# ScalarE copies the weights' high halves, and rotations, pool sums and three half projections take new places in a two-layer decoder trunk

## What is computed

```
h = rmsnorm(x); z = h @ w_in            # rq rk rv rg | pu | mq mk mv mo mi mf
y_ret  = silu(rg) * head_norm(retention(rope(rq), rope(rk), rv))   # 6 heads of 64
y_pool = (windowed mean of pu, widths 2 4 8 16, minus pu) @ w_pool # 4 groups of 64
y_ml   = sigmoid(mo) * head_norm(mlstm(conv(mq, mk), mv, mi, mf))  # 4 heads, 8 chunks
x = x + [y_ret, y_pool, y_ml] @ w_out
x = x + (silu(g) * u) @ w_down          # g, u = rmsnorm(x) @ w_gate_up
x = x + sigmoid(rmsnorm(x) @ w_ple_gate) * (p @ w_ple_proj)
```

## Time and profile before

| | us |
|---|---|
| time, median of 3 runs (range) | 2586.88 (2586.88 to 2587.53) |
| the profiled execution's own time | 2588.19 |
| its span, first to last instruction | 2586.4 |
| TensorE busy in the span | 2499.7 |
| VectorE busy | 1459.0 |
| GpSimd busy | 1288.7 |
| ScalarE busy | 713.5 |
| mean granted TensorE clock | 0.985 |

### The profile page before, as it was taken

The page is one execution under the profiler, slowest core; times in us unless marked ns, Lnnn a source line. Parts: engine busy times, 40 slices in busy tenths (PEclk is TensorE's granted clock), DMA queues, the critical chain, the costliest instruction groups (busy, mean ns, idle before and its releaser), DMA issues.

```text
span 2586.4 us, 29552 instructions
## 1 busy us (share of the span) xinstructions
PE 2499.7 (97%) x11844; PEld 2061.5 (80%) x11844; DVE 1459.0 (56%) x1746; ACT 713.5 (28%) x1091; POOL 1288.7 (50%) x739
## 2 busy tenths in 40 slices
PE   7999998999999999999899999899999999999996
PEld 5887876888888888887778878678888888888885
DVE  6977747663334362354776876677434333534546
ACT  4110114343333330014222021323333333211232
POOL 4423322468788764444434323323787887544430
PEclk9999998999999999999999999999999999999998
DMA  4322222122222352211132112221222323422111
GB/s 154 94 61 54 67 66 92 41 90 74 82 90 74 88 197 105 75 49 49 47 122 83 49 45 71 77 69 62 72 84 79 93 74 97 162 104 78 49 42 65
DMA packets 62904, 208.64 MB, mean 81 GB/s; under 512 B 8872, under 2 KB 17320, under 8 KB 58416
## 3 DMA queue, kind: packets, MB, share of 16 engines
q1 hardware_dynamic: 32544, 116.41, 14.9%
q10 hardware_dynamic: 30224, 90.35, 10.1%
HBM read 161.08 MB, written 32.54 MB: 75 GB/s over the span
## 4 chain that ended last, share of the span: by engine, by line
PE 93%; DVE 4%; ACT 1%; issue 1%; POOL 0%; DMA 0%; ACTq 0%; DVEq 0%
PE proj L1735 19%; PE proj L1736 19%; PE proj L1737 19%; PE proj L1829 5%; PE proj L1830 5%; PE proj L1831 5%; PE aux L1829 5%; PE aux L1830 5%; PE aux L1831 5%; PE aux L1962 1%; PE aux L1971 1%; DVE ret_t L898 1%; PE aux L1873 1%; PE aux L2028 1%; PE aux L1952 0%
## 5 line engine op out<-in xcount | busy, mean ns | idle before, releaser
L1682 POOL TENSOR_TENSOR w_hi<-w_raw,zero 128x1024 fp32r<-128x1024 f32 (+1 forms) x145 | 278.1, 1918 | 1057.3 <-PE proj L1737 1046.1
L1735 PE MATMUL proj<-h_hi,w_hi 128*128 128x512 f32 x1792 | 712.9, 398 | 28.2 <-DVE h_lo L601 17.0
L1736 PE MATMUL proj<-h_hi,w_lo 128*128 128x512 f32 x1792 | 701.6, 392 | 0.0
L1737 PE MATMUL proj<-h_lo,w_hi 128*128 128x512 f32 x1792 | 701.6, 392 | 0.0
L1735 PEld LDWEIGHTS proj<-h_hi,w_hi 128*128 128x128 f32 x1792 | 338.8, 189 | 104.4 <-issue 28.9
L1686 POOL TENSOR_TENSOR w_lo<-w_raw,w_hi 128x1024 fp32r<-128x1024 f32 (+1 forms) x145 | 390.2, 2691 | 11.4
L1737 PEld LDWEIGHTS proj<-h_lo,w_hi 128*128 128x128 f32 x1792 | 338.6, 189 | 71.6
L1736 PEld LDWEIGHTS proj<-h_hi,w_lo 128*128 128x128 f32 x1792 | 339.1, 189 | 70.7 <-issue 2.9
L971 DVE TENSOR_TENSOR x<-x,proj 128x512 f32<-128x512 f32 x128 | 87.7, 687 | 315.0 <-PE proj L1737 315.0
L1693 POOL TENSOR_TENSOR w_lo<-w_raw,w_hi 128x512 fp32r<-128x512 f32 x120 | 183.6, 1531 | 97.5 <-ACT w_hi L1283 97.5
L1693 POOL TENSOR_TENSOR w_lo<-turns,w_hi 128x512 fp32r<-128x512 f32 x120 | 180.4, 1504 | 62.9 <-ACT w_hi L1283 62.9
(11 more groups left out here) (271 smaller groups left out, 4296.3 us busy)
## 6 DMA issues: line engine op xcount, KB each, us to landing
w_raw<-weights SPq DMA_DIRECT2D x170, 512.0 KB, 3.6
act_spill<-act ACTq DMA_DIRECT2D x44, 512.0 KB, 5.5
turns<-weights SPq DMA_DIRECT2D x40, 512.0 KB, 4.3
h_whole<-act_spill ACTq DMA_DIRECT2D x12, 1024.0 KB, 8.8
ffn_b_whole<-act_spill ACTq DMA_DIRECT2D x8, 1024.0 KB, 6.0
ret_t<-ret_qkv ACTq DMA_DIRECT2D x48, 128.0 KB, 3.9
w_raw<-weights SPq DMA_DIRECT2D x16, 384.0 KB, 3.0
x<-x_in ACTq DMA_DIRECT2D x8, 512.0 KB, 8.6
```

The source lines that it names most:

```text
L1682: g.tensor_tensor(whi[:, slot, 0:n], w, zero1[:, 0:1].to_broadcast([P, n]), ALU.add).then_inc(w_hi_made, 1)
L1735: pe.matmul(out, wh, rhi, start=first, stop=False)
L1736: pe.matmul(out, wl, rhi, start=False, stop=False)
L1737: return pe.matmul(out, wh, rlo, start=False, stop=final)
```

## The change

Four edits, in both layers:

1. **High parts of the weights on ScalarE** (in the diff `units_high`). From the fourth unit of the first layer on, ScalarE copies raw weights to `w_hi`; GpSimd waits for that copy and only subtracts. The copies stand at fixed places in ScalarE's list, mostly two units ahead of TensorE.
2. **Halves around the last chunk.** The first retention projection's first half goes between `ml_a 7` and `ml_b 7`, its second behind `ml_b 7`, and the halves of the next units move up behind it.
3. **Rotations taken apart.** `rope` becomes `rope_q`, `rope_k` (the products) and `rope_add` (the sums of k). Those of pair p+1 stand among the items of pair p: q behind `state`, k behind `ret_y`, the sums ahead of `spread`. Their products for pairs 1 and 2 go through `rows` instead of the retention's own tiles. ScalarE's eight swap DMAs a pair become four and four, those of k ahead of ScalarE's squares in `ret_y`.
4. **Pool sums in parts.** Both parts of the first group stand after the last mLSTM item; the two parts of the second group stand in pair 0, in `turn` and `scores`; `pool` stands behind `state 0`. The tile `pool_t` becomes `rows`. `early_high` goes from ahead of `turn 2` to behind it.

```diff
+        u = U_MO + n + 1 if n < NCH - 1 else U_RET
+        m += [("ml_a", n), ("half", u, 0), ("ml_b", n), ("half", u, 1)]
+    m += [("gate_funcs",), ("ml_norm",), ("half", U_RET + 1, 0), ("ml_fin",), ("half", U_RET + 1, 1),
+          ("pool_sum", 0, 0), ("pool_sum", 0, 1), ("half", U_RET + 2, 0), ("rope_q", 0), ("half", U_RET + 2, 1),
+          ("rope_k", 0), ("rope_add", 0)]
     for p in range(PAIRS - 1):
+        for i, step in enumerate(("", "turn", "scores", "state", "ret_y", "spread")):
+            if step == "spread":
+                m.append(("rope_add", p + 1))
             m.append((step, p))
+            if p == 0 and step in ("turn", "scores"):
+                m.append(("pool_sum", 1, ("turn", "scores").index(step)))
+            if p == 0 and step == "state":
+                m.append(("pool",))
+            if step == "state":
+                m.append(("rope_q", p + 1))
+            if step == "ret_y":
+                m.append(("rope_k", p + 1))
...
-    m += [("rope", p), ("half", U_OUT - 1, 1), ("early_high",), ("turn", p), ("early_low", 0), ("scores", p),
+    m += [("half", U_OUT - 1, 1), ("turn", p), ("early_high",), ("early_low", 0), ("scores", p),
...
+            def units_high(L, last):
+                while told[0] <= UNITS * L + last and told[0] < UNITS * DEPTH:
...
+                    for key in {k for k in held if k is not None}:
+                        a.wait_ge(*consumed(key))
+                    a.wait_ge(raw_landed[raw_slot], value)
+                    a.activation(whi[:, slot, 0:n], raws[raw_slot][:, 0:n], ACT.Copy).then_inc(unit_hi.sem, 1)
+                    told[0] += 1
...
                         highs_ahead(L, k + 6)
+                        if last and i in (3, 5, 6):
+                            units_high(L, U_DN + {3: 0, 5: 1, 6: 2}[i])
...
                 a.wait_ge(unit_done.sem, unit_done.at(L, U_PROJ))
+                units_high(L, U_GATE)
                 for c, h in PLE_PIECES[8:]:
...
+                    if what == "unit" or what == "half" and args[1] == 0:
+                        units_high(L, args[0] + 2)
...
+                        if p < PAIRS - 1:
+                            a.wait_ge(vec_step.sem, mark_at(L, ("roped", p + 1, 0, 1)))
+                            swap_halves(L, p + 1, 1, r_swap)
...
-                g.tensor_tensor(whi[:, slot, 0:n], w, zero1[:, 0:1].to_broadcast([P, n]),
-                                ALU.add).then_inc(w_hi_made, 1)
-                highs[0] += 1
-                g.wait_ge(w_hi_made, highs[0])
+                if UNITS * L + u < RING:
+                    g.tensor_tensor(whi[:, slot, 0:n], w, zero1[:, 0:1].to_broadcast([P, n]),
+                                    ALU.add).then_inc(w_hi_made, 1)
+                    highs[0] += 1
+                    g.wait_ge(w_hi_made, highs[0])
+                else:
+                    g.wait_ge(unit_hi.sem, unit_hi.at(L, u + 1))
```

More of the change, by code:

```diff
@@ L271, in build @@
         rows = sb("rows", [P, 2, S])
+        r_cos, r_swap = rows[:, 0, :], rows[:, 1, :]
+        pool_t = rows
         small = sb("small", [P, 64])
@@ L882, in _, with turn_parts, turn_add, k_parts @@
             T0, QR, KR, QX, VT, KZ, SC0 = rw
-            def rope(L, p):
-                b = p % 2
-                if p == 0:
+            def turn_parts(L, p, which, to, other):
+                u = U_RET + 3 * p + which
+                v.wait_ge(emptied[bank(u, 0)].sem, emptied_at(L, u, 0))
+                v.wait_ge(emptied[bank(u, 1)].sem, emptied_at(L, u, 1))
+                v.tensor_tensor(to, rqkv[:, p % 2, which, :], cosT[:, :], ALU.mult).then_inc(vec_step.sem, 1)
+                count()
+                v.wait_ge(swapped[which].sem, swapped[which].at(L, 64 * p + 64))
+                v.tensor_tensor(other, other, sinT[:, :], ALU.mult).then_inc(vec_step.sem, 1)
+                v.wait_ge(vec_step.sem, step_at(L, ("parts", p, which)))
+            def turn_add(L, p, which, dst, one, other):
+                for h in range(2):
+                    v.tensor_tensor(dst[:, hs(h)], other[:, hs(h)], one[:, hs(h)], ALU.add).then_inc(vec_step.sem, 1)
+                    v.wait_ge(vec_step.sem, step_at(L, ("roped", p, which, h)))
+            def k_parts(p):
+                return (r_cos, r_swap) if p > 0 else (T0[:, :], QX[:, :])
+            def rope_k(L, p):
+                turn_parts(L, p, 1, *k_parts(p))
+            def rope_add(L, p):
+                if p > 0:
+                    v.wait_ge(aux_done.sem, aux_at(L, ("rv", p - 1, 1)))
+                turn_add(L, p, 1, KR, *k_parts(p))
+            def rope_q(L, p):
+                if p > 0:
+                    v.wait_ge(vec_step.sem, mark_at(L, ("q_xi", p - 1)))
+                else:
                     v.wait_ge(trig_spread, 64)
@@ L890, in rope @@
                         v.wait_ge(turns_back, 16)
[L891 to L898, removed]
-                    v.wait_ge(vec_step.sem, step_at(L))
-                    for h in range(2):
-                        v.tensor_tensor(dst[:, hs(h)], other[:, hs(h)], T0[:, hs(h)], ALU.add).then_inc(vec_step.sem, 1)
-                        v.wait_ge(vec_step.sem, step_at(L, ("roped", p, which, h)))
+                one, other = (r_cos, r_swap) if p > 0 else (KZ[:, :], SC0[:, :])
+                turn_parts(L, p, 0, one, other)
+                turn_add(L, p, 0, QR, one, other)
             def turn(L, p):
@@ L1403, in _, with swap_halves @@
             by = "p (n c) -> p n c"
[L1405 to L1413 removed]
+            def swap_halves(L, p, which, to):
+                u = U_RET + 3 * p + which
+                for h in range(2):
+                    a.wait_ge(emptied[bank(u, h)].sem, emptied_at(L, u, h))
+                for r in range(0, P, 32):
+                    o = r ^ 32
+                    a.dma_start(to[o:o + 32, :], rqkv[r:r + 32, p % 2, which, :]).then_inc(swapped[which].sem, 16)
             for L in range(DEPTH):
@@ L1620, in _ @@
                         for k in range(16):
+                            if k == 8:
+                                units_high(L, U_GATE + 1)
                             out(k)
```

94 lines of the change are left out of this document (52 added, 42 removed).

## The result

| | before | changed |
|---|---|---|
| median of 4 runs (range), us | 2587.14 (2586.88 to 2587.53) | 2572.14 (2569.70 to 2573.49) |
| profiled execution's span | 2586.4 | 2567.7 |
| VectorE busy | 1459.0 | 1236.7 |
| GpSimd busy | 1288.7 | 984.6 |
| ScalarE busy | 713.5 | 851.5 |

The ratio is 0.9941 (0.9924 to 0.9958). Forecast was 2580.9 with a range of 2564 to 2593: the sign and the range held, the size was 15 where I had 6. Run again, five more times, the same kernel had a median of 2576.12 (2568.18 to 2578.77), ratio 0.9955 (0.9941 to 0.9969). So the gain is 11 to 15 us, and the changed kernel spreads over some 10 us, the one before over 3.4.

A forecast was written before the change was run, and what follows sets the result against it. TensorE, busy 2499.7 of 2586.4 us, bounds the kernel, so only its waits and half-clock stretches can change. Gains 41.2 less new waits 26.2 less clock 9.0 make 6.0: 2582.2 profiled, 2580.9 median, range 2564 to 2593.

The forecast's parts named there:

- Chunk 7: Last mLSTM chunk: a half covers TensorE's 5.03 wait and the clock stays up; gain 16.2 us in both layers.
- Pair 1's turn: Retention pair 1: k rotated earlier, so the 1.79 wait and 0.5 in the transposes go; gain 4.6 us, both layers.
- Pair 2: Retention pair 2: k ready, `early_high` comes last, `state` starts at 13.8 instead of 22.4; gain 17.2 us, both layers.
- Layer change: Start of second layer: VectorE's last split no longer slowed by GpSimd; TensorE waits 3.2 us less, once.
- New waits: Added waits at ml_fin 1.9, turn 0 3.4, pool 2.9, down projection 3.8, embedding 1.1: 13.1 a layer, 26.2 us.
- Turn 0: First retention turn: VectorE's row of work, with two GpSimd subtractions in it, is late; 3.4 us a layer.
- Down projection: Second unit's copy stands behind six activations on ScalarE, so its low part comes late; 3.8 us a layer.
- Clock: TensorE's half clock behind new waits and `out_part` behind pair 2, by a straight line: 4.5 a layer, 9.0 us lost.
- waits as counted, no clock lost: Rival: new waits come as forecast but the clock stays up, 9.0 come back; 2572 us, chance 0.20.
- The rival in which GpSimd beside VectorE costs nothing: GpSimd's subtractions fall beside ScalarE's or TensorE's work and VectorE keeps pace; 8.8 a layer less, 2563 us, chance 0.15.
- The rival of late swaps: k's rotation still waits for DMAs or `ret_y` squares, gains of pairs 1 and 2 shrink; 2598 or 2589 us, chance 0.08.
- the slower one: Many short waits: clock falls at ml_fin, turn 0, pool and down projection, 3.2 apiece; 2596 us, chance 0.14.

The follow-up runs named there:

- no_half7: Changed kernel with the halves around chunk 7 put back as before, all else as changed; 2581.36 us, ratio to before 0.9976.
- half7_only: Kernel before with only the halves moved around chunk 7; pool sums, rotations and GpSimd's high parts as before; 2588.72 us, ratio to before 1.0005.
- after_again: The changed kernel run a second time, nothing altered, with its own profile; 2576.12 us, ratio to before 0.9955.
- copy_behind: Changed kernel with the weight copy in front of pair 2's fourteen high parts put behind them; 2566.15 us, ratio to before 0.9916.
- k_back: Changed kernel with k's rotation (products and sums) of pairs 1 and 2 back behind spread; 2586.17 us, ratio to before 0.9994.
- copies_late: Changed kernel with two of ScalarE's weight copies held back, so GpSimd's subtractions fall behind VectorE's work at ml_fin and turn 0; 2567.94 us, ratio to before 0.9924.
- best: Changed kernel with pool products ahead of state 0, four weight copies moved or held back, pair 1's q swap behind the pool's copies; 2540.18 us, ratio 0.9817.

## Why the prediction was right in sign and too small

- **Chunk 7, 16.2.** The wait and its slow clock went, as said. But calling that a gain of the halves was wrong by half: of each 5.03, 2.76 was GpSimd in VectorE's way (no_half7), and the halves alone gain nothing (half7_only). That the price held was luck: two causes were at work where I saw one.
- **Pair 1's turn, 4.6.** As said: no wait.
- **Pair 2, 17.2.** Measured 15.9, with clock in it that the forecast counted apart: `state` came 14.7 after turn 2 could begin, and 13.4 in the first layer of after_again, where the clock stayed at 1.00; I had 13.8. The step named as last was the last: high parts, held by a copy and a subtraction (copy_behind). k_back shows that k's early rotation carries it.
- **Layer change, 3.2.** Measured 3.3.
- **New waits, 26.2.** The term that was most off. Measured 18.5. Turn 0: I put 3.4, it is 1.37 and 0.36 in the transposes, 1.7; I had 4.8 us of GpSimd in VectorE's row, and it cost 2.1 at a small copy (2.24 for 0.17) and 1.5 at a product, since each subtraction had begun beside an instruction of VectorE that was under way. Down projection: 3.8, measured 3.2 and 2.0. ml_fin: 1.9, measured 1.2. Pool 2.9 and embedding 1.1: 2.7 and 0.95. All these erred to the dear side, 7.7 together.
- **Clock, 9.0.** Measured outside pair 2: 6.4 in the profiled execution, at other places than said: none at ml_fin and turn 0, one at the down projection (first layer), one at the pool (second), and two at the embedding, which I hadn't listed. With some 1.2 a layer in pair 2 it is 8.8 in all. A straight line between a wait of 1.79 and one of 5.03 gave a fair sum, but not for its reason: in between the same wait may cost 1.7 or nothing. That the sum fits is luck.
- **Not foreseen.** 1.3 for a wait of 0.64 at the start of each layer's feed-forward part, and 1.3 of clock at the layer change.

In the order of new waits, clock, not foreseen, start and pair 2, 7.7 + 2.6 + 2.6 + 0.9 - 1.3 = 12.5 make up the 12.7 between the forecast 6.0 and the profiled 18.7. The rival "waits as counted, no clock lost" had 2572, the number that came, but by luck: the waits were smaller than it said and the clock was lost. The rival in which GpSimd beside VectorE costs nothing (2563) is refuted by the 6.04 and 2.70 and by copies_late. The rival of late swaps is refuted by turn 1 and 2 without waits, the slower one by six new waits at ml_fin, turn 0 and the pool of which one brought the clock down.

## What to carry to other kernels

Before work is moved in front of a wait, ask whether the engine that is waited for gets its work done any sooner: half7_only took 5 us from one wait and gave 6.6 to four others. When work goes to an engine with slack, its place in that engine's list is all that counts: with four of some 70 copies a layer moved, on top of the pool's products and one swap, the merge was worth 22 us, before that nothing. And when GpSimd and VectorE both work on tensors in SBUF, look for what GpSimd does during VectorE's critical group before taking the group's length as its own.

## What the hardware did that I had not expected

The clock's answer to a wait isn't a function of its length alone: behind 2.74 us it fell in one layer and not in the other of the same execution, behind 3.3 us in one execution and not in the next, and behind 0.89 and 1.22 close together it fell in both layers of half7_only. The changed kernel, with several such waits, spreads more (10.6 us over nine runs, against 3.4 over fifteen of the kernel before; 3.5 over four of best, too few to compare), so a difference of 3 us between two of them needs the profile beside the times. GpSimd's subtraction doesn't add its length to VectorE's row: 2.64 of it cost the eight scalings 2.2, and 2.54 cost a product 1.5. Its 2.90 cost a copy of 64x2 that it met 2.1 (2.24 for 0.17).
